# Rounding each weight tile and taking its rest in two halves of 1024 columns

## The reference

```python
def first_block(x, ...):
    for i in range(2):
        h = _multiscale_pool(x, ...) if i == 0 else _diff_attention(x, ...)
        x = _layernorm(ALPHA * x + h, ...)
        x = _layernorm(ALPHA * x + (silu(x @ w_gate[i]) * (x @ w_up[i])) @ w_down[i], ...)
    return x

def second_block(x, ...):
    x = x + token_mixer(rms_norm(x, ...), ...)
    x = x + square(relu(rms_norm(x, ...) @ w_up)) @ w_down
    return rms_norm(x, final_norm_g)
```

## Time and profile before

| | |
|---|---|
| runs of the kernel before | 1013.52 us median of 3 (1010.97 to 1014.65) |
| profiled execution | 1013.57 us, span of the core 1011.0 us |
| mean granted TensorE clock | 0.996 |
| busy: PE, DVE, ACT, POOL | 97%, 68%, 45%, 4% of the span |
| chain of waits, by engine | PE 76%, DVE 11%, issue 5%, ACT 5%, DMA 1%, POOL 1% |
| moved by DMA | 175.21 MB, mean 173 GB/s |

### The profile page before, as it was taken

How to read it: one execution, slowest core, us unless ns; L and a number is a source line. 1 busy time by engine, 2 the same in 40 slices (tenths; PEclk the granted TensorE clock), 3 DMA queues, 4 the chain that set the end, 5 groups by cost and what they waited for, 6 DMA issues and landing times.

```text
span 1011.0 us, 15349 instructions
## 1 busy us (share of the span) xinstructions
PE 979.7 (97%) x6035; PEld 866.9 (86%) x6035; DVE 691.8 (68%) x866; ACT 455.7 (45%) x583; POOL 39.1 (4%) x52
## 2 busy tenths in 40 slices
PE   8899999999999999999999999999999989999997
PEld 7778888888897788888888879899999878888886
DVE  3777676677786778667668477785776566666664
ACT  2544344344565434444434446564653453434342
POOL 2000001000002000000001000000000000000000
PEclk9999999999999999999999999999999999999999
DMA  8566676638642357555642754544565535555541
GB/s 289 161 222 211 204 227 209 207 125 224 177 142 91 119 188 240 189 196 185 204 141 68 219 152 126 156 137 126 167 208 170 191 122 184 179 196 198 176 166 41
DMA packets 142166, 175.21 MB, mean 173 GB/s; under 512 B 7089, under 2 KB 121178, under 8 KB 142118
## 3 DMA queue, kind: packets, MB, share of 16 engines
q1 hardware_dynamic: 138592, 165.50, 50.9%
q0 software_dynamic: 2560, 8.69, 2.8%
q10 hardware_dynamic: 966, 0.35, 0.1%
HBM read 173.43 MB, written 1.09 MB: 173 GB/s over the span
## 4 chain that ended last, share of the span: by engine, by line
PE 76%; DVE 11%; issue 5%; ACT 5%; DMA 1%; POOL 1%; ACTq 1%; SPq 0%; DVEq 0%; POOLq 0%
PE bank L483 75%; DVE w_lo L961 4%; ACT w_hi L953 2%; DVE x_both L1340 1%; DVE arena L1412 1%; DMA raw<-w_up 1%; ACT x_both L991 1%; DVE arena L1329 1%; PE bank L723 1%; ACT arena L983 1%; POOL rstd L1890 1%; DVE x_rows L1380 1%; DVE x_rows L1373 0%; ACTq L1208 0%; POOL rstd L1837 0%
## 5 line engine op out<-in xcount | busy, mean ns | idle before, releaser
L961 DVE TENSOR_TENSOR w_lo<-raw,w_hi 128x2048 fp32r<-128x2048 f32 (+1 forms) x156 | 351.4, 2257 | 152.8 <-ACT w_hi L953 152.3
L483 PE MATMUL bank<-x_both,w_hi 128*128 128x256 f32 (+1 forms) x2128 | 441.2, 331 | 7.9 <-DVE x_both L1340 4.0
L483 PEld LDWEIGHTS bank<-x_both,w_hi 128*128 128x128 f32 x2128 | 358.7, 190 | 50.5 <-issue 12.6
L953 ACT ACTIVATE w_hi<-raw 128x2048 fp32r<-128x2048 f32 (+1 forms) x157 | 294.6, 1880 | 117.9 <-PE bank L483 110.5
L483 PE MATMUL bank<-x_both,w_lo 128*128 128x256 f32 x1520 | 288.0, 283 | 0.8 <-DVE arena L1412 0.8
L483 PEld LDWEIGHTS bank<-x_both,w_lo 128*128 128x128 f32 x1520 | 230.5, 191 | 4.5 <-issue 1.1
L483 PE MATMUL bank<-w_hi,arena_r 128*128 128x512 f32 x608 | 171.5, 390 | 2.8 <-DVE w_lo L961 1.6
L483 PEld LDWEIGHTS bank<-w_hi,arena_r 128*128 128x128 f32 x608 | 112.9, 188 | 27.2 <-DVE w_lo L961 2.5
L483 PE MATMUL bank<-w_lo,arena_r 128*128 128x512 f32 x304 | 95.7, 389 | 0.0
L1412 DVE TENSOR_REDUCE arena<-bank 128x512 f32<-128x1024 f32 x57 | 69.6, 1222 | 24.5 <-PE bank L483 24.5
L483 PE MATMUL bank<-w_hi,x_both 128*128 128x512 f32 x256 | 75.2, 393 | 2.2 <-DVE w_lo L961 0.9
(11 more groups left out here) (149 smaller groups left out, 671.4 us busy)
## 6 DMA issues: line engine op xcount, KB each, us to landing
raw<-w_up SPq DMA_DIRECT2D x76, 512.0 KB, 4.6
raw<-w_down SPq DMA_DIRECT2D x76, 512.0 KB, 4.2
raw<-w_in SPq DMA_DIRECT2D x60, 512.0 KB, 4.5
raw<-w_gate SPq DMA_DIRECT2D x44, 512.0 KB, 4.7
raw<-w_qkv SPq DMA_DIRECT2D x24, 512.0 KB, 4.6
raw<-w_o SPq DMA_DIRECT2D x16, 512.0 KB, 4.2
table<-bias_vectors POOLq DMA_DIRECT2D x12, 256.0 KB, 4.9
raw<-w_pa SPq DMA_DIRECT2D x4, 512.0 KB, 4.3
```

Source lines behind the costliest of these rows:

```text
L483: return nc.tensor.matmul(*a, skip_group_check=True, **k)
L953: last = nc.scalar.activation(o, i, ACT.Copy)
L961: last = nc.vector.tensor_tensor(o, i, h.bitcast(F32), ALU.subtract)
```

## The change

ACT rounds a whole unit with two activations of 1024 columns, each of which counts `hi_done` up by 1, so that a unit now stands for 2 in this count. DVE takes the rest with two subtractions of 1024 columns; the first waits for the first count of its unit, the second for the second. `lo_done` still counts units and is raised after the second. The indexer's unit keeps its pieces and adds 2 at once. POOL's subtraction for unit 0 stays one instruction and waits for both halves.

```diff
@@ round_unit
-            for o, i in split_views(slot, indexer)[0]:
-                last = nc.scalar.activation(o, i, ACT.Copy)
-            last.then_inc(hi_done, 1)
+            if indexer:
+                for o, i in split_views(slot, indexer)[0]:
+                    last = nc.scalar.activation(o, i, ACT.Copy)
+                last.then_inc(hi_done, 2)
+                return
+            for h in range(2):
+                c = slice(h * UW // 2, (h + 1) * UW // 2)
+                nc.scalar.activation(w_hi[slot][:, c], raw[slot][:, c], ACT.Copy).then_inc(hi_done, 1)
@@ rest_unit
-            eng.wait_ge(hi_done, unit + 1)
-            his, los = split_views(slot, indexer)
-            for (h, _), (o, i) in zip(his, los):
-                last = nc.vector.tensor_tensor(o, i, h.bitcast(F32), ALU.subtract)
+            if indexer:
+                eng.wait_ge(hi_done, 2 * unit + 2)
+                his, los = split_views(slot, indexer)
+                for (h, _), (o, i) in zip(his, los):
+                    last = nc.vector.tensor_tensor(o, i, h.bitcast(F32), ALU.subtract)
+            for h in range(0 if indexer else 2):
+                eng.wait_ge(hi_done, unit * 2 + (h + 1))
+                c = slice(h * UW // 2, (h + 1) * UW // 2)
+                last = nc.vector.tensor_tensor(w_lo[slot][:, c], raw[slot][:, c], w_hi[slot][:, c].bitcast(F32),
+                                               ALU.subtract)
             last.then_inc(lo_done, 1)
@@ block.gpsimd
-            eng.wait_ge(hi_done, 1)
+            eng.wait_ge(hi_done, 2)
```

## The result

The changed kernel takes **1005.52 us** in the median of 5 runs (1004.32 to 1005.64), against 1013.52 for the kernel before (now 5 runs, 1010.97 to 1014.65): a ratio of 0.9922, interval 0.9906 to 0.9938. The miss of the time is narrow; that of the sum, 4.8 against 7, is not. The profiled execution of the changed kernel took 1004.32 us, with a span of 1002.3.

The account below looks back on a forecast made before the run. TensorE, busy 97% of the span, was taken as the bound. Terms -0.71 - 0.48 - 0.79 + 0.06 - 0.89 - 1.39 - 0.69 + 0.12 = -4.77 us took 1013.57 to 1008.8 us; range 1005.8 to 1012.5.

Parts of the forecast that it names:

- the handovers named: Places where TensorE waits behind ACT rounding a unit and DVE directly taking its rest; each direct handover to gain 0.79 us.
- the waits at 211, 236, 527, 543, 654 and 794: TensorE's waits at both feed-forward ends, V projection, second norm and mixer (times in us); forecast gone or near 0.1.
- the one before the last part: Entry to the last part: TensorE's 2.33 us wait for the bank sum behind two rests, forecast +0.12 us.
- A wait of TensorE can give back no more than it shows: Rule for every gap: the gain at a TensorE wait is capped at the idle time shown there.
- the third wait: Last TensorE wait at each feed-forward entry, for a direct handover: 0.20 us at the first, 0.28 at the second.
- the cap of 1.39: End of second feed-forward part: TensorE's waits 0.48 and 0.91 limit the gain to 1.39, though DVE's chain moves by -1.58.
- I take +0.06: Second root of the attention norm: the forecast's chosen term, +0.06 us, with -0.48 as the other end.
- the forecast's second case: Attention norm's second root: POOL gets in between DVE's halves, DVE waits for it, and the scaling starts when it did before.
- the third case: Attention norm's second root: POOL and DVE both run freely, and 0.48 us would be gained.
- The start's +0.10: Program start: ACT's rounding of unit 1 waits for its load, norm copies stand behind it; +0.10 us for all.
- in the range, not in the sum: Clock: a longer TensorE wait at another gap would cost 1.5 us at lower granted clock; counted only in the range.
- the case of more gain: Rival: 0.95 us a handover and POOL let in freely give -5.9, so 1007.7; span 1004.5 to 1007.7, chance 0.15.

## Why the prediction was wrong

**Right.** The costs of a split: halves 1.05 and 1.22, pairs 2.00 and 2.36 (2.00 and 2.35 forecast), handover 3.44 (3.43). The places: all of the gain but the norm's is at the handovers named, the loops give nothing beyond their first turn (140.10 us in both), the V projection gives 0.76 (0.79), the waits at 211, 236, 527, 543, 654 and 794 are gone or at most 0.11, the one before the last part is longer by 0.13 (0.12).

**The step that failed first: "A wait of TensorE can give back no more than it shows".** A wait that ends wholly gives back more. Idle time in the profile runs from the end of one product's record to the start of the next, and the record of a product of 512 columns is 0.39 long while such products start 0.23 apart. The ends are modelled, as the profile's page says. The last product ahead of a wait thus still stands as busy for 0.16 that the waiting costs as well, and behind a wait the next product starts 0.31 after the first and not 0.23. Where the wait of 0.48 was, 210.54 to 211.94 is 1.40; the same products stand 0.68 apart after the change (209.42 to 210.10): 0.72 for a shown 0.48. Counted in the same way the 0.41 at 654.67 cost 0.52, the 0.28 at 794.92 cost 0.51 and the 0.20 at 64.34 cost 0.47. A wait that only gets shorter gives back what it shows, to 0.02: at the V projection 0.89 became 0.11 and the shift was 0.76, and the bank sum ahead took the wait before the last part from 2.46 to 1.41, a shift of 1.05.

By stretch, what was gained beyond the sum is 0.30 (-1.11 against -0.81) + 0.26 + 0.29 + 0.19 + 0.37 = 1.4 us of the missing 2.3. In the entries it comes from the third wait; what the first gave beyond its 0.39 was taken up by the middle one, where DVE decides. At the end of the second part the cap of 1.39 was what was wrong: the shift is the 1.58 that the forecast had for DVE's chain, and a wait of 0.07 is left.

**The second: the root of the attention norm, "I take +0.06".** The root gave 0.62 to 0.65, and its row of the table 0.77: POOL's operation took 2.55 and not 3.62, and the wait of 0.48 behind it ended. POOL got in at the middle, as the forecast's second case had it; what that case assumed beside it, that DVE's second half would wait for POOL, didn't happen. So the price of the third case, -0.48, was the right one, short of the full size by the step above.

The start's +0.10 was 0.00 in this pair of traces. No run can confirm or refute it, as the start moves by up to 2 us from execution to execution (33.27 to 35.29). With the 0.8 of the norm, the 1.4 of the waits and this 0.1 the missing 2.3 us are complete.

**The clock, "in the range, not in the sum".** Leaving it out of the sum was right: it explains 1.57 of the 8.7 us between the two spans, and the 7 us between first products and last entry are without it. But it widens what a median of a few runs can say, by more than the rests of the sum; that 1005.52 fell outside the range and 1005.95 inside is chance of that size. The low end, 1005.8, was short because the case of more gain put part of its extra into larger handovers, which didn't come, and took the same cap at every wait. Its other part, the root's 0.48, did come.

## What to carry to other kernels

A handover between two engines is worth cutting only where a wait of the bounding engine stands behind it: 66 us of DVE's idle time went, 7 us of the kernel's. Price a wait of TensorE by the starts of the products around it, less their usual spacing, and not by the idle time that the profile shows: here each that ended wholly was worth 0.1 to 0.3 us more, and each that only got shorter what it showed. Compare traces from a product behind the start on, as the start and the clock move a run's time by more than such a wait. And before cutting an operation, see whether one that the bounding engine waits for stands behind one that nobody waits for yet: moving three bank sums up was worth another 4 us between medians, of which the traces show 2.6.

## What the hardware showed that was not expected

- **POOL let in between two DVE operations, and DVE not held.** Before, POOL's operation ended 1.50 behind the end of DVE's whole rest (323.57 to 325.07). With halves it ended at 321.28, which is 1.50 behind the end of the *first* half (318.56 + 1.22 = 319.78). DVE's two halves took 2.36 together, as at 44.50 where POOL is idle. All five traces with a whole rest there have 3.62, all eight with halves 2.55, and all thirteen have 1.67 at the norm's first root (294.52 before), where a rest of DVE begins only as it ends. So the first of DVE's operations held POOL up, and the second ran while POOL did. The Trainium skill, "SBUF — State Buffer", section "SBUF: two separate sides", has the one that starts first block the other for its whole instruction; the first half fits that, the second doesn't, and here the measurement decides. Why the second isn't held no run here shows.
- **TensorE's clock falls by chance.** Behind waits of 2.3 to 2.5 us before the last part, 16 products took 5.3 to 5.5 us in four traces and 3.9 in five, at a granted clock of 0.70 and 1.00 in the windows read: part of the stretch ran at 1.2 instead of 2.4 GHz. The changed kernel did both, in two traces of the same program; both traces of the unchanged one have the fall. Behind 1.41 us it fell in none of four traces. Once the first products behind the start were slow too, behind 3.54 idle us: 8 of them took 3.22 (one unit whole at the ends) where they take 2.08 after the change.
- **A second operation in a row costs less than the fixed part of a single one.** Two halves on DVE take 0.07 more than the whole, where an estimate from the Trainium skill, "VectorE: DVE Perf Modes", section on the TRN2 errata, is 0.16: its (N + 151)/0.96 ns with the fixed part paid twice. A single half at 1.22 agrees with that formula, the pair doesn't, and the measurement decides. The records of two in a row overlap by 0.08.
